# A one-column write, waited for, in the middle of each head's gathers

## The reference

```python
q = (hb @ w_q).reshape(PEER_BLOCK, PEER_HEADS, 2, PEER_HALF)      # 128 tokens at a time, 8 heads
sc = jnp.einsum('thcd,hcnd->thcn', q, sub_keys).astype(jnp.float32)
s1, i1 = lax.top_k(sc[:, :, 0], PEER_TOPK)                          # 16 best keys of each half
s2, i2 = lax.top_k(sc[:, :, 1], PEER_TOPK)
...
top_s, pos = lax.top_k(cand_s, PEER_TOPK)                           # 16 best pairs of keys
idx = jnp.take_along_axis(cand_i, pos, axis=-1)
g = jax.nn.softmax(top_s, axis=-1)
u = u_tab[idx]                                                      # rows of a 16384 x 1024 table
act = jax.nn.gelu(jnp.einsum('thkd,td->thk', u, hb))
wts = (g * act.astype(jnp.float32)).astype(hb.dtype)
v = v_tab[idx]                                                      # rows of a second such table
return jnp.einsum('thk,thkd->td', wts, v)
```

## Time and profile before

| what | us |
|---|---|
| median of 3 timed runs | 2285.29 |
| lowest and highest of them | 2284.11, 2286.78 |
| span of the profiled execution | 2379.3 |

### The profile page before, as it was taken

The page is one execution under the profiler, slowest core; times in us unless marked ns, Lnnn a source line. Parts: engine busy times, 40 slices in busy tenths (PEclk is TensorE's granted clock), DMA queues, the critical chain, the costliest instruction groups (busy, mean ns, idle before and its releaser), DMA issues.

```text
span 2379.3 us, 27257 instructions
## 1 busy us (share of the span) xinstructions
PE 2070.6 (87%) x9038; PEld 1171.1 (49%) x9039; DVE 979.9 (41%) x2276; ACT 555.0 (23%) x1027; POOL 497.6 (21%) x562
## 2 busy tenths in 40 slices
PE   8998998967658576584999989999999999999998
PEld 7867887623223232232678854444444444444443
DVE  5955555646647566473375232111111111111112
ACT  4636301212112111122214222211111111121112
POOL 0000003466666666665300000000000000000000
PEclk9999999988878787896999989999999999999999
DMA  7352586799999999998842428799999999999996
GB/s 301 142 212 80 195 356 262 277 368 344 370 380 344 366 364 353 371 345 327 345 180 107 176 97 372 301 429 429 428 428 428 430 428 428 429 429 428 428 429 280
DMA packets 111703, 784.34 MB, mean 330 GB/s; under 512 B 13056, under 2 KB 13312, under 8 KB 80160
## 3 DMA queue, kind: packets, MB, share of 16 engines
q1 hardware_dynamic: 37920, 515.18, 52.3%
q0 software_dynamic: 73728, 268.47, 29.8%
HBM read 782.55 MB, written 1.05 MB: 329 GB/s over the span
## 4 chain that ended last, share of the span: by engine, by line
PE 75%; issue 11%; DVE 5%; another core or an unknown queue 2%; ACT 2%; POOL 2%; DMA 1%; DVEq 0%; ACTq 0%; POOLq 0%; SPq 0%
PE ps L786 56%; PE ps L945 16%; PE ps L1210 1%; DVE ring L1942 1%; DVE arena L1942 1%; DMA arena<-in_peer_v,arena 1%; PE ps L918 1%; POOL ring L746 1%; POOL ring L744 1%; DMA ring<-in_peer_v,arena 1%; DVE arena L1700 0%; DVE arena L1891 0%; ACT arena L1372 0%; PE ps L1241 0%
## 5 line engine op out<-in xcount | busy, mean ns | idle before, releaser
L786 PE MATMUL ps<-ring,arena 128*64 128x512 f32 (+2 forms) x3336 | 749.5, 589 | 41.8 <-issue 41.7
L786 PEld LDWEIGHTS ps<-ring,arena 128*64 128x64 f32 (+1 forms) x3336 | 262.9, 140 | 501.5 <-issue 500.7
L945 PE MATMUL ps<-ring,arena 128*128 128x512 f32 x768 | 366.5, 635 | 156.8 <-issue 134.7
L786 PE MATMUL ps<-arena,ring 128*128 128x256 f32 (+1 forms) x2272 | 486.2, 373 | 3.8 <-DVE arena L1685 3.2
L786 PEld LDWEIGHTS ps<-arena,ring 128*128 128x128 f32 x2272 | 417.4, 189 | 65.5 <-issue 6.9
L945 PEld LDWEIGHTS ps<-ring,arena 128*128 128x128 f32 x768 | 154.9, 204 | 364.6 <-issue 340.0
L945 PE MATMUL ps<-arena 128*128 128x512 f32 (+2 forms) x600 | 211.3, 599 | 66.5 <-ACT arena L1278 50.6
L1942 DVE CUSTOM_DVE_ANT_0 ring<-ring,ps 128x1024 f32<-128x1024 f32 x192 | 228.1, 1218 | 94.8 <-DMA ring<-in_peer_v,arena 88.5
L1600 ACT COPY arena<-ps 128x512 f32<-128x512 f32 (+1 forms) x165 | 89.2, 541 | 739.6 <-PE ps L786 683.5
L2255 DVE TENSOR_TENSOR arena<-ps,arena 128x512 f32<-128x512 f32 x66 | 45.7, 692 | 438.4 <-PE ps L1210 438.4
L786 PE MATMUL ps<-arena 128*128 128x128 f32 (+4 forms) x1502 | 215.2, 298 | 11.1 <-ACT arena L1262 6.6
(11 more groups left out here) (336 smaller groups left out, 1214.5 us busy)
## 6 DMA issues: line engine op xcount, KB each, us to landing
ring<-in_w_exp SPq DMA_DIRECT2D x192, 2048.0 KB, 17.1
ring<-in_w_in SPq DMA_DIRECT2D x24, 2048.0 KB, 9.5
ring<-in_w_ada SPq DMA_DIRECT2D x12, 2048.0 KB, 8.8
ring<-in_w_out SPq DMA_DIRECT2D x4, 2048.0 KB, 8.2
ring<-in_w_peer_q SPq DMA_DIRECT2D x4, 2048.0 KB, 10.6
ring<-in_w_br_rnn SPq DMA_DIRECT2D x4, 1280.0 KB, 7.4
ring<-in_w_br_attn SPq DMA_DIRECT2D x2, 2048.0 KB, 13.9
ring<-in_peer_u,arena POOLq DMA_INDIRECT x192
```

Of the source, the lines that this page charges most:

```text
L786: return pe.matmul(o, l, r, start=start, stop=stop)
L945: return pe.matmul(o, l, r, start=start, stop=False, skip_group_check=True)
```

## The change

In the turn of `k` that is half of 16 (`k == 8`), ahead of that row's wait for PE and its two gathers, POOL writes zeros into the first column of `iota_i` (128 partitions, one element each, the value that it holds from the start) and waits for that write to be done. The count per turn of the loop grows from 2 * (2 + 16) to 2 * (3 + 16), since each head now has one more counted instruction. It happens 16 times in all.

```diff
             for tile in range(TT):
-                per = 2 * (2 + TOPK)
+                per = 2 * (3 + TOPK)
                 with pool.Fori(0, PH // 2) as i:
...
                             if k == 3:
                                 A.filled(pool, "ss2")
+                            if k == TOPK // 2:
+                                own(pool.memset(iota_i[:, 0:1], 0.0))
                             own.mark(pool.wait_ge(s_pv, i * (2 * TOPK) + TOPK * g + k + 2))
```

## The result

The changed kernel takes 2295.3 us (median of 7 runs, 2291.89 to 2300.77), the kernel before 2286.8 in the same comparison (7 runs, 2284.11 to 2289.67). The ratio is 1.0035 with a 95% interval of 1.0024 to 1.0046: **8.0 us slower** (5.5 to 10.5). The profiled execution of the changed kernel has a span of 2293.0 us.

The account below looks back on a forecast made before the run. POOL's gather issue was taken to bound the PEER stage at 40.65 us a head, transfers close behind at 41.0; 14 heads x 0.6 us = 8.4 us on 2285.3 gave 2294 us, range 2283 to 2299.5.

Parts of the forecast that it names:

- the 94 us: Profiled span over median timed run (2379.3 against 2285.29); taken as mostly the profiler's own, lying in POOL's PEER-stage waits.
- The price: POOL's added time at row 8 for the write and its wait: 0.10 + 0.97 - 0.30 = 0.77 us a head.
- The low bound of 0.04: Least cost of the pause, from a one-column write at the program's start: 0.34 us between gathers for 0.30.
- The heads that pay: Heads in which the pause lies on the path: 14 of 16, the first two covered by POOL's waits for PE.
- The first head's cover: POOL's waits of 6.48 and 10.98 us for PE after row 8 in the first head make the pause disappear.
- The middle of 0.6 us a head: Between POOL alone setting the pace (0.77) and transfers setting it before (0.42): 14 x 0.6 = 8.4 us.
- The hidden pause: Rival, 27%: POOL's waits at row 12, or slower transfers, absorb the pause; time stays at 2285, 2284 to 2288.
- The faster kernel: Rival, 12%: the pause in POOL's gathers lets DVE in and ends its idle early; 27 us gained, 2258.
- The figure of 358 GB/s: Rule on HBM-SBUF transfers: a head would take 46.9 us, hiding the pause, so 0 instead of 8.4 us.

Follow-up runs that it names:

- the second profile: The kernel before, unchanged, profiled once more: 2289.1 us against 2288.9, profiled span 2289.4 us where the first profile had 2379.3.

## Why the prediction was right

**The assumption at its base held.** The prediction took "without proof" that the 94 us were not in the timed runs and that POOL there issues with hardly a wait. It had the reason wrong: it put them down to the profiler, but the second profile, taken in the same way, lacks them. The second profile has a span of 2289.4 us, some 3.5 us of waits in 14 heads, and heads of 40.98 us on average from copy to copy (the third to the fifteenth), little more than the 40.65 that POOL needs by the prediction's sum. Had the waits been in the timed runs, the pause would likely have gone into them, as it does in the kernel with one gather.

**The price** was put at 0.77 us, from the head's start, with the write of the earlier trace rows; it is 0.69 in most heads and 0.80 in three. The nearest row was the right one: the same successor behind a wait for an own instruction. The low bound of 0.04, from a write that an ordinary instruction waits for the earlier trace rows, is far off. The gap behind the write was to be 0.97 and is 0.88 or 0.99 (1.27 in the first head, where it is covered).

**The heads that pay** were counted as 14; they are 15. The second head's waits of 2.73 and 2.81 us belonged to the disturbed profile; in the second one its pitch goes from 41.7 us before to 42.4 after, so it pays. The first head's cover is real: 51.4 us before, 51.3 after, with a wait for PE of 10.45 us before and 9.38 after.

**The middle of 0.6 us a head** gave 8.4 us against 8.0 measured, but it is right only as a sum, and by luck; this is the step that failed in its working. The prediction let the transfers hide up to 0.35 us of the pause in every head, by their 41.0 us against POOL's 40.65. Then a head should have grown by 0.42 us if the transfers set the pace, and by 0.6 in the middle. In the profiles it grew from 40.98 to 41.82, by 0.84, and POOL's groups have 11.3 us in 14 heads: within the stage the transfers hide nothing. From the first gather to the end of the last, the pause adds 12.1 us with full rows and 12.8 with half of `v` (666.9 to 679.8), where the transfers have room: the same price. What the transfers do is fall behind by a few us in the course of the stage; the pauses take that lag away, which is worth some 3 to 5 us once, at the end. Eleven to twelve less three to five came out near to 14 x 0.6.

**The rivals.** The hidden pause falls with the kernel before: there were hardly any waits to hide it. Its mechanism was sound, as the two kernels with one gather show. The faster kernel falls too: DVE's idles of 9.45 and 25.48 us without a visible cause are not in the second profile, where the longest of that kind at that line is 0.2, so there was nothing to let in. The figure of 358 GB/s in the Trainium skill, page "DMA: Bandwidth & Descriptors", section "Where 436 GB/s comes from", under which the sum was 0, is passed by the stage's 409 GB/s, and by the 422 with one gather.

What stays open is the exact split of the 3 to 5 us at the end: the shorter way of row 11 accounts for 2.0 to 3.6 of them, and the rest is within the 2.5 us by which profiles of like kernels differ. Open is also the cause of the 1.61 us wait between two gathers: the four profiles of kernels with two gathers a row and pauses in the first tile each have one such (1.60 to 1.62 us), and the five without such pauses have none.

## What to carry to other kernels

A wait for an engine's own last instruction is not priced by the instruction: here the write alone and the wait alone were free, and the two together cost 0.7 us each time, paid in full within the stage because that engine's issue set its pace. Before a profile's waits are taken for cover, set its span against the timed median; where it is some per cent longer, profile once more, since the waits may be of that execution alone. And where an engine that makes descriptors sets the pace, fewer and larger gathers can win: one gather of 8 KB rows for two of 4 KB took 18 us off here, with the higher rate of the larger rows, and hid the pause as well.

## What the runs showed of the hardware

A gather of 128 rows costs POOL 0.94 us and 0.30 to the next whatever its rows hold: 2, 4 and 8 KB rows have mean busy times of 937 to 955 ns in the groups shown. Between two gathers POOL has 0.30 us in which a short write of its own (0.12) runs for nothing; what opens that gap no view shows. The gathers moved 409 GB/s with rows of 4 KB and 422 with rows of 8 KB, with the DMA engines busy throughout and gathers queued in both (10.4 us and some 25 to land, against 4.6 with half rows), so the larger rows were worth 3% in rate beside what they saved on POOL.
